# Last output tile of each sub-layer split by token half, its normalisation started inside the tile; conditioning groups in pairs

## What is computed

```python
def rms_norm(x, g=None):
    y = xf * lax.rsqrt(jnp.mean(jnp.square(xf), axis=-1, keepdims=True) + EPS)
...
def swiglu(h, w1, w3, w2):
    return (jax.nn.silu(h @ w1) * (h @ w3)) @ w2
def modulated_pre(x, g, mods, j):
    return rms_norm(x, g) * (1.0 + mods[:, 3 * j + 1, None]) + mods[:, 3 * j, None]
def gated_post(x, o, g, mods, j, coef):
    return x + coef * mods[:, 3 * j + 2, None] * rms_norm(o, g)
...
mods = (jax.nn.silu(c) @ ada_w[l] + ada_b[l]).reshape(c.shape[0], 3 * N_SUB, D_MODEL)
h = modulated_pre(x, norm_pre[l, 0], mods, 0)
x = gated_post(x, swiglu(h, ffn_w1[l, 0], ffn_w3[l, 0], ffn_w2[l, 0]), norm_post[l, 0], mods, 0, 0.5)
```

## Time and profile before

| | us |
|---|---|
| median of 3 runs (lowest to highest) | 2380.72 (2378.61 to 2381.71) |
| the profiled execution, its own time | 2378.93 |
| its span | 2377.1 |
| TensorE busy in the span | 2311.3 |
| GpSimd, ScalarE, VectorE busy | 878.9, 808.5, 1234.7 |
| turn T0, T1, T2, T3, T4 | 31.7, 29.0, 28.6, 31.8, 29.3 |

### The profile page before, as it was taken

One profiled execution on the slowest core, in us unless ns is written; L12 is line 12 of the kernel. 1 busy time (PEld: TensorE's weight loads), 2 busy tenths in 40 slices (PEclk: granted clock), 3 DMA queues, 4 the chain that ended last, 5 costly groups with the idle time before them and its releaser, 6 DMA issues.

```text
span 2377.1 us, 44378 instructions
## 1 busy us (share of the span) xinstructions
PE 2311.3 (97%) x17736; PEld 2195.5 (92%) x17736; DVE 1234.7 (52%) x2091; ACT 808.5 (34%) x1332; POOL 878.9 (37%) x382
## 2 busy tenths in 40 slices
PE   8999999999999999999999999999999999999997
PEld 7999999899558999999999999998994699999997
DVE  5333379867471433338143333996856524333561
ACT  3322232333454423332243333224343543333321
POOL 1333444334113344434434434443431153333353
PEclk8999999999999999999999999999999999999999
DMA  6222268322211122236312223782231022222552
GB/s 232 89 88 88 83 236 295 141 89 80 73 36 54 63 84 84 88 129 241 107 60 84 88 88 121 272 271 100 80 111 51 1 71 71 88 88 88 190 200 73
DMA packets 73240, 272.05 MB, mean 114 GB/s; under 512 B 8960, under 2 KB 10368, under 8 KB 72640
## 3 DMA queue, kind: packets, MB, share of 16 engines
q1 hardware_dynamic: 73152, 270.84, 33.1%
HBM read 267.36 MB, written 3.45 MB: 114 GB/s over the span
## 4 chain that ended last, share of the span: by engine, by line
PE 70%; issue 16%; DVE 6%; POOL 3%; DMA 2%; ACT 2%; SPq 1%; DVEq 0%; POOLq 0%; ACTq 0%
PE ps L661 19%; PE ps L665 19%; PE ps L662 19%; POOL w_lo L540 3%; DVE wide_v L1454 2%; PE ps L671 2%; DMA ada_w<-in_ada 2%; PE ps L701 1%; PE ps L703 1%; PE ps L1025 1%; PE ps L910 1%; PE ps L1048 1%; PE ps L992 1%; PE ps L998 1%; DMA ada_first<-in_ada 1%
## 5 line engine op out<-in xcount | busy, mean ns | idle before, releaser
L540 POOL TENSOR_TENSOR w_lo<-raw,w_hi 128x1024 fp32r<-128x1024 f32 (+1 forms) x304 | 785.6, 2584 | 1349.9 <-ACT w_hi L1118 956.9
L661 PE MATMUL ps<-h_hi,w_hi 128*128 128x272 f32 x3296 | 887.4, 289 | 7.7 <-POOL w_lo L540 7.7
L662 PE MATMUL ps<-h_lo,w_hi 128*128 128x272 f32 x3296 | 889.2, 287 | 0.0
L665 PE MATMUL ps<-h_hi,w_lo 128*128 128x272 f32 x3296 | 685.7, 289 | 0.0
L661 PEld LDWEIGHTS ps<-h_hi,w_hi 128*128 128x128 f32 x3296 | 619.1, 188 | 10.5 <-POOL w_lo L540 10.3
L662 PEld LDWEIGHTS ps<-h_lo,w_hi 128*128 128x128 f32 x3296 | 620.9, 188 | 0.2
L1118 ACT CAST w_hi<-raw 128x1024 fp32r<-128x1024 f32 (+1 forms) x236 | 268.6, 1138 | 837.1 <-PE ps L665 753.1
L665 PEld LDWEIGHTS ps<-h_hi,w_lo 128*128 128x128 f32 x3296 | 519.2, 188 | 0.0
L661 PE MATMUL ps<-u_hi,w_hi 128*128 128x272 f32 x1408 | 381.2, 288 | 3.8 <-POOL w_lo L540 3.8
L662 PE MATMUL ps<-u_lo,w_hi 128*128 128x272 f32 x1408 | 380.2, 288 | 0.0
L1454 DVE CUSTOM_DVE_ANT_0 wide_v<-ada_w,ps 128x1024 bf16<-128x1024 f32 x288 | 332.2, 1218 | 47.5 <-DMA ada_w<-in_ada 29.4
(11 more groups left out here) (256 smaller groups left out, 2382.3 us busy)
## 6 DMA issues: line engine op xcount, KB each, us to landing
raw<-in_w_up SPq DMA_DIRECT2D x176, 512.0 KB, 3.4
ada_w<-in_ada SPq DMA_DIRECT2D x144, 512.0 KB, 5.0
raw<-in_w_dn SPq DMA_DIRECT2D x64, 704.0 KB, 5.3
raw<-in_w_mix SPq DMA_DIRECT2D x64, 512.0 KB, 3.5
ada_first<-in_ada SPq DMA_DIRECT2D x10, 512.0 KB, 8.0
decay<-in_decay SPq DMA_DIRECT2D x2, 2048.0 KB, 9.8
ada_first<-in_ada_first SPq DMA_DIRECT2D x6, 512.0 KB, 11.4
x<-in_x SPq DMA_DIRECT2D x4, 544.0 KB, 16.4
```

Of the source, the lines that this page charges most:

```text
L540: pool.tensor_tensor(w_lo[:, slot, 0:width], raw[:, slot, 0:width], w_hi[:, slot, 0:width].bitcast(F32), ALU.subtract).then_inc(lo_done.se ...
L661: pe.matmul(ps[:, bank + t, 0:width[t]], wh, hi[:, n], start=start, stop=False)
L662: pe.matmul(ps[:, bank + t, 0:width[t]], wh, lo[:, n], start=False, stop=False)
L665: last = pe.matmul(ps[:, bank + t, 0:width[t]], wl, hi[:, n], start=False, stop=stop)
```

## The change

The last output tile is computed half by half: all 22 (or 8) weight tiles for tokens 0 to 271, then for tokens 272 to 543. The sums, the root, the reciprocal and the spread are made for each half. Those of the first half stand inside the products of the second half, the sums ahead of weight tile 2 and the spread ahead of weight tile 6; those of the second half stand inside the next stage's first tiles. VectorE updates `x` in half rows and does all of it, with the products in PSUM; the low rows `h_lo` are still made whole, behind all half rows. GpSimd, in place of its adds to `x`, adds the squares of rows 0 to 3 of `x`, and TensorE sums the result once (`early_sum`) beside rows 4 to 7, five sums in place of eight. `acc` has two buffers, the loops of the conditioning groups go two groups at a time, a group waits for the `columns` of the group before the last, and the first two groups are written out. The last ffn1 computes only the two groups that it uses.

```diff
-TOK_AT = [0, P, 2 * P, 3 * P, T - P]
+TOK_AT = [0, P, HT - P]
...
+N_EARLY = 4
+SQ = N_EARLY + KD - 1
+SUMS = KD - N_EARLY + 3
...
-            def add_odd(l, j, m):
-
-                pool.wait_ge(x_prod.sem, x_prod.at(l, j * KD + m + 1))
-                pool.tensor_tensor(x[:, m, :], x[:, m, :], tmp_v[:, 1, :], ALU.add).then_inc(x_new[1].sem, 1)
+            def add_x_squares(l, j, m):
+
+                pool.wait_ge(x_sq.sem, x_sq.at(l, j * KD + m + 1))
+                if m == 1:
+                    pool.tensor_tensor(squares[:, :], tmp_s[:, 0, :], tmp_s[:, 1, :], ALU.add).then_inc(sq_added.sem, 2)
+                else:
+                    pool.wait_ge(sq_added.sem, sq_added.at(l, j * SQ + m))
+                    pool.tensor_tensor(squares[:, :], squares[:, :], tmp_s[:, m % 2, :], ALU.add)\
+                        .then_inc(sq_added.sem, 1)
...
+            def half_sums(l, j, t):
+
+                if t == 0:
+                    pe.wait_ge(sq_added.sem, sq_added.at(l, (j + 1) * SQ))
+                    if j != 1:
+                        pe.wait_ge(ada_done.sem, ada_done.at(
+                            l, 2 * (ADA_A if j == 0 else ADA_A + (ADA_B if l < DEPTH - 1 else KD))))
+                token_sums(squares[:, :], t, True, False)
...
+                token_sums(tmp_s[:, 1, :], t, False, True).then_inc(sums.sem, 1)
...
+                    for k in range(KD):
+                        if w == 0 and k == (0 if j == 2 else 1):
+                            half_sums(*post, 1)
+                        if w == 0 and k == 5:
+                            spread(*post, 1)
...
-                        if w == 0:
-                            pre_sum(l, j, k)
+                        if w == 0 and k % 2:
+                            if k == KD - 1:
+                                last.then_inc(w_used.sem, 1)
+                            pre_sum(l, j, 4 + k // 2)
+                    if w == 0:
+                        early_sum(l, j)
...
+            def last_tile(l, j, chunk0, per_tile, chunk_tiles, operand):
...
+                for t in range(2):
+                    n = slice(t * HT, (t + 1) * HT)
+                    for q in range(per_tile):
+                        if t == 0:
+                            pe.wait_ge(lo_done.sem, lo_done.at(l, n0 + q + 1))
+                        for kk in range(chunk_tiles):
+                            k = q * chunk_tiles + kk
+                            if t and k == 2:
+                                half_sums(l, j, 0)
+                            if t and k == 6:
+                                spread(l, j, 0)
...
-                        by_dve = m % 2 == 0 or m == KD - 1
-                        prod = tmp_v[:, 1, :] if m % 2 else along(6)
-                        v_.tensor_tensor(prod, o_buf[:, m, :], along(4), ALU.mult).then_inc(x_prod.sem, 1)
...
+                    for t in range(2):
+                        n = slice(t * HT, (t + 1) * HT)
+                        invert(t)
+                        dve.wait_ge(inv_spread.sem, inv_spread.at(l, 2 * j + t + 1))
+                        for m in range(KD):
...
+                            v_.tensor_tensor(prod, o_buf[:, m, n], ps[:, 4 + t, 0:HT], ALU.mult).then_inc(x_prod.sem, 1)
+                            dve.wait_ge(x_prod.sem, x_prod.at(l, c))
+                            v_.tensor_tensor(x[:, m, n], x[:, m, n], prod, ALU.add).then_inc(x_new.sem, 1)
...
-                        dve.wait_ge(columns.sem, columns.at(l, cols))
+                        dve.wait_ge(columns.sem, columns.at(l, cols - 2))
...
-                    with dve.Fori(2, ADA_A // ADA_RING) as i:
-                        ada_group(l, i, 16 + i * ADA_RING, i * ADA_RING, i * 2 + 2, first_ffn=True)
+                    with dve.Fori(1, ADA_A // (2 * ADA_RING)) as i:
+                        for b in range(2):
+                            ada_group(l, b, i * 2 + b, 16 + i * (2 * ADA_RING) + b * ADA_RING, i * (2 * ADA_RING) + b * ADA_RING,
+                                      i * 4 + (2 * b + 2), first_ffn=True)
```

More of the change, by code:

```diff
@@ L276, in streaming_trunk @@
         c_placed = signal("c_placed", 2)
-        x_prod = signal("x_prod", 24)
-        x_new = [signal(f"x_new{i}", 12, 4) for i in range(2)]
+        x_prod = signal("x_prod", 48)
+        x_new = signal("x_new", 48)
         x_sq = signal("x_sq", 24)
@@ L479, in ffn @@
                     ada_tile(0, t)
+                last = s == 1 and l == DEPTH - 1
                 with sp.Fori(1, 4 - s) as i:
-                    down(i)
+                    down(i, ada=not last)
                 if s == 1:
@@ L561, in turn_over @@
                     low(l, chunk + k, k, KD * P)
-                if l or j:
-                    for m in range(1, KD - 1, 2):
-                        add_odd(*((l, j - 1) if j else (l - 1, 2)), m)
+                for m in range(1, N_EARLY):
+                    add_x_squares(l, j, m)
                 for k in range(2):
@@ L690, in first_tiles @@
             def first_tiles(l, j, chunk):
+                post = (l, j - 1) if j else (l - 1, 2)
                 if (l, j) == (0, 0):
                     first_high(chunk)
+                for w in range(2 if l or j else 0):
+                    pe.wait_ge(lo_done.sem, lo_done.at(l, chunk + w + 1))
+                    for k in range(KD):
[4 more added lines that the diff above has]
+                        if w == 0:
+                            pe.wait_ge(h_high.sem, h_high.at(l, high_count(l, j, 0, k)))
+                        pe.matmul(ps[:, 2 * w, 0:HT], w_hi[:, w, k * P:(k + 1) * P], h_hi[:, k, 0:HT],
+                                  start=k == 0, stop=False)
+                        pe.matmul(ps[:, 2 * w, 0:HT], w_lo[:, w, k * P:(k + 1) * P], h_hi[:, k, 0:HT],
+                                  start=False, stop=False)
@@ L765, in out_tiles @@
                 tile(1, 1, True)
-                with pe.Fori(1, KD // 2) as i:
+                with pe.Fori(1, KD // 2 - 1) as i:
                     tile(i * 2, 0, False)
                     tile(i * 2 + 1, 1, False)
-                pe.wait_ge(sq_added.sem, sq_added.at(l, (j + 1) * SQ))
-                if j != 1:
-                    pe.wait_ge(ada_done.sem, ada_done.at(l, 2 * (ADA_A if j == 0 else ADA_A + ADA_B)))
-                token_sums(squares[:, :], 4, True, False)
-                pe.wait_ge(out_sq.sem, out_sq.at(l, (j + 1) * KD))
@@ L775, in out_tiles @@
-                token_sums(tmp_s[:, 1, :], 4, False, True).then_inc(sums.sem, 1)
-                spread(l, j, 4)
+                tile(KD - 2, 0, False)
+                last_tile(l, j, chunk0, per_tile, chunk_tiles, operand)
+            def last_tile(l, j, chunk0, per_tile, chunk_tiles, operand):
+                pe.wait_ge(out_ev.sem, out_ev.at(l, j * KD + KD - 2))
+                n0 = chunk0 + (KD - 1) * per_tile
+                last_k = per_tile * chunk_tiles - 1
+                for t in range(2):
[9 more added lines that the diff above has]
+                                spread(l, j, 0)
+                            hi, lo = operand(k)
+                            slot = (n0 + q) % 2
+                            wh, wl = (w[:, slot, kk * P:(kk + 1) * P] for w in (w_hi, w_lo))
+                            pe.matmul(ps[:, 2 + t, 0:HT], wh, hi[:, n], start=k == 0, stop=False)
+                            pe.matmul(ps[:, 2 + t, 0:HT], wh, lo[:, n], start=False, stop=False)
+                            last = pe.matmul(ps[:, 2 + t, 0:HT], wl, hi[:, n], start=False, stop=k == last_k)
+                        if t:
+                            last.then_inc(w_used.sem, 1)
+                    if t == 0:
+                        last.then_inc(half_mm.sem, 1)
+                if l == DEPTH - 1 and j == 2:
+                    half_sums(l, j, 1)
+                    spread(l, j, 1)
@@ L1801, in mixer @@
                 heads_low(len(ITEMS) - 1)
-            for k in range(KD):
-                v_.memset(scratch[:, 4 + k:5 + k], 0.0).then_inc(x_new[k % 2].sem, 1)
             for v in range(2):
```

286 lines of the change are left out of this document (168 added, 118 removed).

## The result

The changed kernel takes 2383.72 us (median of 20 runs, 2380.31 to 2386.91), the kernel before 2379.72 in as many: a ratio of 1.0016, 95% interval 1.0010 to 1.0023. It is slower by 3.9 us. The forecast was 2391, 10.2 us slower. The direction was right, and the time lies in the range, but the size was less than half of the one forecast.

The account below looks back on a forecast made before the run. TensorE, busy 97% of the span, bounds the kernel, so time is gained where it idles, in the turns between stages; 3.7 + 1.4 - 1.4 + 5.9 + 1.1 - .9 + .4 = +10.2 us gave 2391, range 2377 to 2403.

Parts of the forecast that it names:

- Conditioning in T0 and T3: Turns after ffn0, layers 0 and 1: first-half sums wait for conditioning, with 60 products queued behind; +3.7 and +5.9 us.
- The walk of the groups: Conditioning groups followed one by one against GpSimd's subtractions: dots end at 442.8 and 1613.0, gains 2.7 and .6 us.
- The tail: End of each turn, after the low rows: last pair of products, cast, low part and hand-overs, 4.2 us.
- T2's chain: Turn after ffn1 in layer 0, without conditioning: steps from the seventh tile's end sum to 43.85 against 45.25, -1.4 us.
- T1 and T4: Turns after the mixer, layers 0 and 1: short tile hides nothing, VectorE's first half bounds; +1.4 and +1.1 us.
- The rival in which the clock falls in T1, T2 and T4 too: Pairing gives nothing or meets more subtractions, and TensorE's clock drops in three more turns: +5 to +9 us, chance .15.
- The port term: Low rows of each turn: VectorE stands still during GpSimd's adds of squares, sharing SBUF ports; 3.4 us a turn.
- the hand-over: Allowance in the low rows of each turn: 16 instructions in 6.68 us, taken as 6.9 with it.
- The first rival: No port wait in the low rows: 2.2 of 3.4 us come back in each of five turns, -11, 2380; chance .15.
- what does pairing give: Conditioning groups: six of twelve gaps become short and the first are written out, some 3.5 us, part lost again.
- The rival on the faster side: Conditioning ends in time, by 436.9 in T0: -4.5 and -4.6 for both ffn0 turns, total 2372; chance .10.

## Why the prediction was right and wrong

- *Conditioning in T0 and T3* (forecast +3.7 and +5.9, measured +5.6 and +3.7). The mechanism was right: 7.8 and 5.8 us of idle with 60 products behind it, forecast 5.9 and 8.1. The clock fell as forecast: 5.4 us from sums to spread against 5.3. The walk of the groups had pairing gain 2.7 us in T0 and .6 in T3. Counted from t6, the dots were done after 18.3 us in both before, and after 17.6 in T0 and 15.6 in T3 in the changed kernel: gains of .7 and 2.7, the other way round. That the two errors cancel in the sum is luck. In T0 the same code of the groups ended after 15.6 in four of the runs above and after 17.6 in the changed kernel; what decides between the two is open. The tail in T0 and T3 was 4.85 and not 4.2: the second fall of the clock, which the forecast did not have.
- *T2's chain* held step by step: 9.7 to the sums (forecast 9.7), 2.85 (2.9), 8.6 (8.7), 7.9 (8.0). T1 and T4 likewise, each some .2 shorter ahead of the sums. The rival in which the clock falls in T1, T2 and T4 too overlooked the kernel before: its granted clock is .50 in all three already (783 to 789, 1199 to 1205, 1950 to 1956), and the turns read from its trace held that price.
- **The port term was too large.** "I take 3.4": it measured 2.8, and with the .2 I had added for the hand-over a turn spent 9.5 us in the place of 10.3. Five turns make 4 us of the forecast's surplus. GpSimd's first add ends just as the low rows begin, so less of the three falls into them than 2.5. That rule of the Trainium skill (SBUF — State Buffer, "SBUF: two separate sides") is borne out in kind: the half rows, with one operand in PSUM, keep their .44 beside the first add, and the low rows, with two in SBUF, are held until an add ends (1.84 in place of .74).
- *The first rival's price was wrong too.* "2.2 of 3.4 come back": without the adds all 2.8 came back in each turn, and more in T0 and T3, since VectorE is the slower side of five sums as long as the clock holds. The forecast had put TensorE 1.2 us behind the low rows; two low rows and a sum take it 1.42 us against 1.65 on VectorE. With eight sums nothing comes back.
- **The step that failed outright is "what does pairing give".** I priced the pairs only at the end of the dots. I never asked who waits for the first two groups. ScalarE does, and behind it the third weight chunk, four times .95 us. The row stood in the trace of before, as an idle of TensorE outside the turns. So the forecast had this at nothing, and it is worth 3.8 us. In the profiles the miss is 10.2 less 3.8, 6.4 us: these 3.8, and 3.5 in the turns, where the port term alone was 4 too large and the other errors nearly cancel, and .2 at the start, less the mixer's 1.6, which belong to one execution. The remaining half microsecond is not placed.
- *The rival on the faster side* did not come true: the dots ended 7.8 us after TensorE first asked, far from the 436.9 that it needed. That TensorE need not ask so early was shown instead: with the sums behind the tile it does not wait for the same dots at all.

## What to carry to other kernels

A wait that moves into the middle of a block of work holds up everything queued behind it: ask first when each thing that it waits for comes, and split only where all come in time (here ffn1, not ffn0 nor the short tile of the mixer). When several edits come together, price each one alone and in both directions: the small one (pairs, -6 us) was hidden by the large one (+10 us). And for an edit that makes something ready earlier, list all who wait for it, the first consumer and not only the last; the way to find them is every idle row of the bounding engine over the whole span, not only those in the place that the change speaks of.

## What the runs showed of the hardware

A loop on VectorE in place of the same two groups written out cost it .85 us up to `mul_post` (.62 us of idle between the groups against .13), and showed up as a .95 us wait of TensorE, through two other engines. Moving three GpSimd instructions of 1.36 us from beside VectorE's instructions with a PSUM operand to beside those with two SBUF operands cost VectorE 2.8 us, which in this kernel is just what it saved TensorE in three sums of .92. The third of these adds was longer too, 1.61.

The granted clock differs between executions of the same code. One more stretch at .50 made some 1.6 us, in the retention part (a gap of 11.05 against 9.5) and in T2 (34.7 against 33.1 from the first sums). Such a difference between two profiles is not yet one between two kernels: compare the granted clock of the same stretch first.
